# The last down-projection unit and the final norm, computed in two token halves

## The chip, the cores and the metric

The kernel runs on one core of a Trainium2 chip. The number that counts is device time in microseconds, as the median of several runs. TensorE is called PE in the rows (PEld is its weight load), VectorE DVE, ScalarE ACT, GpSimd POOL and the queue that issues the DMAs SP. A name that ends in q (PEldq, DVEq) is the sequencer of that engine.

## The reference

A two-layer encoder trunk on 512 tokens of 1024 features. Each layer ends in a gated MLP whose down-projection is added to the residual `x`; after the second layer there is one more RMSNorm, and its result is the output:

```python
def rms_norm(x, g):
    xf = x.astype(jnp.float32)
    y = xf * lax.rsqrt(jnp.mean(xf * xf, axis=-1, keepdims=True) + EPS)
    return (y * g.astype(jnp.float32)).astype(x.dtype)
...
    for l in range(DEPTH):
...
        h = rms_norm(x, norm_ffn_g[l])
        x = x + conv_ffn(h, ffn_w_up[l], ffn_conv_w[l], ffn_conv_b[l], ffn_w_down[l])
    return rms_norm(x, final_norm_g)
```

## The kernel before

**Layout.** Everything is held with features on the 128 partitions and the 512 tokens along the free dimension: `x` is eight tiles of 128x512. Weights come as packs of four 128x128 tiles through four slots. SP loads `w_raw`, ACT rounds it to `w_hi` (line 516), POOL forms the rest `w_lo` (line 405), and a product is made of three TensorE matmuls per tile pair: `w_hi` with the high part of the input, `w_hi` with its low part, `w_lo` with the high part. All of them go through one helper, line 1106. The inputs of the down-projection are `m_hi` and `m_lo`.

**Units.** A dense unit is one 128-feature output tile, summed in the PSUM bank `dense[n % 2]`. The last down-projection of a layer has eight units of ten weight tiles each, so 30 matmuls of 512 columns per unit. When a unit is done, DVE adds the bank to `x` (line 1087) and counts `evac`; ACT then makes `h_hi` (458) and the square of the tile (466) for the coming norm, and DVE makes `h_lo` (733) and adds the square into `ssq` (741). ACT rounds two more packs after each unit, once the slots' old packs have been consumed; `run_done`, which PE counts at the end of each run of weight tiles, tells it so.

**The layer loop.** Every engine walks through a loop over the two layers (`Fori(0, DEPTH)`), written out at PE line 1178, DVE line 765 and ACT line 506, and jumps back once. Right behind PE's jump come the matmuls of the next layer's first group of units. They wait for the banks: the first for the last unit but one, the second (`dense[1]`) for the last unit's addition.

**The tail.** Behind the loop, PE sums the squares over the features with a matrix of ones: one product for `ssq`, which by then holds tiles 0 to 5, and one each for the squares of tiles 6 and 7, in plain float32 (two passes each), into the bank `M[1]`. ACT turns that into the inverse root by a logarithm and an exponential (lines 477 and 480), DVE scales eight tiles (line 1097), and SP stores each tile as it is ready (line 395). The order is what stands in the code; nothing is scheduled by a planner here.

Of the kernel before, what the change touches and what calls it, by code (L numbers as in the profile page):

```python
# [18 lines left out]
DEPTH = 2  # L19
D, S, P = 1024, 512, 128  # L20
KD = D // P
# [10 lines left out]
SLOTS = 4  # L32
# [53 lines left out]
SEGS, UNIT_END, PACK_END, N_SEGS = segments()  # L86
N_PACKS = len(PACK_END)
SEG0 = 5


SCHEDULE = (
# [103 lines left out]
def build(nc, a, out):  # L195
    f32, f32r = mybir.dt.float32, mybir.dt.float32r
    ALU, ACT, AX = mybir.AluOpType, mybir.ActivationFunctionType, mybir.AxisListType
    with ExitStack() as ctx:
# [109 lines left out]
        bias_loaded, setup_done = sem("bias_loaded"), sem("setup_done")  # L308
        y_ready, stored = sem("y_ready"), sem("stored")

        block = ctx.enter_context(nc.Block())

        def bank(b, parts):
# [8 lines left out]
        def _(sp):  # L322
# [25 lines left out]
            for l in range(DEPTH):  # L348
# [47 lines left out]
            sp.wait_ge(stored, 16 * KD)  # L396


        @block.gpsimd
# [45 lines left out]
        def _(act):  # L445
# [60 lines left out]
            with act.Fori(0, DEPTH) as l:  # L506
# [161 lines left out]
                for half, (g0, ng) in enumerate(HALVES):  # L668
# [35 lines left out]

        @block.vector
        def _(dve):
# [55 lines left out]
                    first_sum(o - 2)  # L762
            dve.wait_ge(c_loaded, 16 * N_CONST_LOADS)
            link(V.tensor_copy(ones_r[:, :], ones[:, :]))
            with dve.Fori(0, DEPTH) as l:
                base[0] = l * DVE_LINKS
                links[0] = 3
                for o in (KD - 2, KD - 1):
                    sum_tile(l * 2, o)
# [287 lines left out]
                for half, (g0, ng) in enumerate(HALVES):  # L1057
                    k0 = links[0]
                    e0 = UNIT_END[U_UP[half] - 1]
                    with dve.Fori(0, ng) as i:  # L1060
                        fi = l * FT + g0 + i
                        if half == 0:
                            dve.wait_ge(rstd_ready, l * 2 + 2)
                        dve.wait_ge(run_done, l * N_SEGS + (SEG0 + e0 + 2) + i * 4)
                        V.tensor_tensor(fpad[:, 2:2 + S], dense[0][:, :], rstd[:, :], ALU.mult).then_inc(evac, 1)  # L1065
                        dve.wait_ge(evac, l * N_EV + (U_UP[half] + 1) + i * 2)
                        dve.wait_ge(f_scaled, fi + 1)
                        ins = V.scalar_tensor_tensor(fy, fpad[:, 1:1 + S], par["fconv"][:, bass.ds(fi * 4 + 1, 1)],  # L1068
                                                     fy, ALU.mult, ALU.add)
# [13 lines left out]
                    links[0] = k0 + ng  # L1083
                    for n in range(U_DN[half], U_DN[half] + 8):
                        o = n - U_DN[half]
                        dve.wait_ge(run_done, l * N_SEGS + (SEG0 + UNIT_END[n]))
                        V.tensor_tensor(x[:, o, :], dense[n % 2][:, :], x[:, o, :], ALU.add).then_inc(evac, 1)  # L1087
                        if half == 1 and o:
                            low_tile(l * 2 + 2, o - 1)
                        if half == 1 and 1 < o < KD - 1:  # L1090
                            sum_tile(l * 2 + 2, o - 1)
                with dve.If(l < DEPTH - 1):
                    low_tile(l * 2 + 2, KD - 1)
                assert links[0] == 3 + DVE_LINKS, links
            dve.wait_ge(rstd_ready, 2 * DEPTH + 1)
            for o in range(KD):
                V.scalar_tensor_tensor(yt[:, o, :], x[:, o, :], par["g"][:, 2 * DEPTH * KD + o:2 * DEPTH * KD + o + 1],  # L1097
                                       rstd[:, :], ALU.mult, ALU.mult).then_inc(y_ready, 1)


        @block.tensor
        def _(pe):
# [75 lines left out]
            with pe.Fori(0, DEPTH) as l:  # L1178
# [297 lines left out]
                for half, (g0, ng) in enumerate(HALVES):  # L1476
                    p0 = SEGS[U_UP[half]][0][0]

                    def up(u, i):

                        runs = [(2 * u + s, l * N_PACKS + (p0 + 2 * u + s) + i * 4, 0, 4 * s, 4) for s in range(2)]
                        unit(u, l * N_EV + (U_UP[half] - 2 + u) + i * 2, runs, *h_src,
                             h_tile(l * 2 + 1) if half == 0 and u == 0 else None)

                    def g_tile(k):

                        if k in (0, ng - 1):
                            pe.wait_ge(f_lo, l * FT + (g0 + ng - 1 + (k > 0)))
                    with pe.Fori(0, ng) as i:
                        if half == 0:  # L1490
                            up(0, i)
                            with pe.If(i < 1):
                                norm(l * 2 + 1, "FNORM", l)
                            up(1, i)
                        else:
                            up(0, i)
                            up(1, i)
                    for n in range(U_DN[half], U_DN[half] + 8):
                        dense_unit(n, m_src(0), g_tile if n == U_DN[half] else None)
            take("NORM", 0, DEPTH)  # L1500
            pe.wait_ge(ssq_added, DEPTH * 14 + KD - 3)
            mm(M[1][:, :], ones[:, :], ssq[:, :], True, False)
            for o in (KD - 2, KD - 1):
                pe.wait_ge(sq_ready, DEPTH * 16 + o + 1)
                ins = mm(M[1][:, :], ones[:, :], sq[:, o % 2, :], False, o == KD - 1)
            ins.then_inc(m_ready[1], 1)

# [145 lines left out]
```

## Time and profile before

| | us |
|---|---|
| median of 3 runs | 1279.43 |
| lowest, highest | 1278.46, 1279.56 |
| the profiled execution's own time | 1278.12 |
| its span, first to last instruction | 1276.2 |
| PE busy / DVE / ACT / POOL, share of the span | 99% / 50% / 45% / 46% |

A row of the timeline has the start in us from the span's beginning, the extent in us, the engine, the line, the instruction, output and inputs, and the number of merged instructions. Matmuls are pipelined, and the extent of one (0.39 us at 512 columns) is longer than the distance to the next, so rates are read from starts.

### The profile page before, as it was taken

What the parts mean: (1) busy time and instruction counts of PE and PEld (TensorE: products, weight loads), DVE (VectorE), ACT (ScalarE), POOL (GpSimd) and SP (SyncE); (2) the same over time, 40 slices, a digit from 0 to 9 for tenths busy, and PEclk for the clock granted to TensorE, in tenths of its full rate; (3) what the DMA queues carried; (4) which work ended last, traced back from release to release, by engine and by line L of the source; (5) the groups of instructions that cost most, each with busy time, mean ns of one, the idle gap of its engine ahead of it and who ended that gap; (6) DMA issues with size and microseconds to landing.
All of it is one profiled execution on the core that took longest, in us unless ns stands there. A gap on an engine that the chain in (4) does not pass through costs nothing.

```text
span 1276.2 us, 21086 instructions
## 1 busy us (share of the span) xinstructions
PE 1257.3 (99%) x6066; PEld 1024.9 (80%) x6066; DVE 638.6 (50%) x962; ACT 571.4 (45%) x910; POOL 588.4 (46%) x438
## 2 busy tenths in 40 slices
PE   7999999999999999999999999999999999999996
PEld 5888878888888888888878887788888888888885
DVE  6859774565544013442248697646645430134423
ACT  6442484564443224443345237754643432244433
POOL 4543432536444445554445335425454444455541
PEclk9999999999999999999999999999999999999999
DMA  6353212233333333333323623313233333333333
GB/s 216 104 151 100 75 57 68 85 89 114 93 97 95 98 95 98 95 95 91 101 84 86 171 67 83 83 47 106 84 111 93 96 99 99 91 99 98 93 96 110
DMA packets 77483, 124.89 MB, mean 98 GB/s; under 512 B 7752, under 2 KB 20456, under 8 KB 77416
## 3 DMA queue, kind: packets, MB, share of 16 engines
q1 hardware_dynamic: 77416, 124.03, 33.8%
q8 instruction: 38, 0.62, 0.2%
q14 instruction: 29, 0.24, 0.1%
HBM read 121.45 MB, written 2.55 MB: 97 GB/s over the span
## 4 chain that ended last, share of the span: by engine, by line
issue 38%; PE 38%; POOL 18%; DVE 2%; POOLq 2%; ACT 1%; DMA 1%; SPq 1%; DVEq 0%; ACTq 0%
PE dense L1106 35%; POOL w_lo L405 18%; PE mix L1106 2%; POOLq L404 1%; POOLq L418 1%; DVE arena L784 1%; DMA w_raw<-in_w 1%; DVE arena L1097 0%; DMA x<-in_xT 0%; ACT h_hi L458 0%; SPq L364 0%; ACT w_hi L516 0%; PE mix L1429 0%; ACT arena L492 0%; SPq L379 0%
## 5 line engine op out<-in xcount | busy, mean ns | idle before, releaser
L405 POOL TENSOR_TENSOR w_lo<-w_raw,w_hi 128x512 fp32r<-128x512 f32 x424 | 579.3, 1381 | 652.1 <-ACT w_hi L516 647.5
L1106 PE MATMUL dense<-h_hi,w_hi 128*128 128x512 f32 x992 | 390.9, 394 | 3.2 <-DVE h_lo L733 2.9
L1106 PE MATMUL dense<-h_lo,w_hi 128*128 128x512 f32 x992 | 386.7, 390 | 0.0
L516 ACT ACTIVATE w_hi<-w_raw 128x512 fp32r<-128x512 f32 x422 | 257.3, 626 | 280.4 <-PE dense L1106 262.5
L1106 PE MATMUL dense<-h_hi,w_lo 128*128 128x512 f32 x992 | 269.9, 390 | 0.0
L1106 PEld LDWEIGHTS dense<-h_hi,w_hi 128*128 128x128 f32 x992 | 186.5, 188 | 45.1 <-issue 5.4
L1106 PEld LDWEIGHTS dense<-h_hi,w_lo 128*128 128x128 f32 x992 | 186.3, 188 | 40.6 <-issue 1.7
L1106 PEld LDWEIGHTS dense<-h_lo,w_hi 128*128 128x128 f32 x992 | 186.5, 188 | 39.5 <-issue 1.4
L1106 PE MATMUL dense<-m_hi,w_hi 128*128 128x512 f32 x544 | 212.9, 391 | 0.0
L1106 PE MATMUL dense<-m_lo,w_hi 128*128 128x512 f32 x544 | 211.8, 389 | 0.0
L1106 PE MATMUL dense<-m_hi,w_lo 128*128 128x512 f32 x544 | 147.7, 389 | 0.0
L1106 PEld LDWEIGHTS dense<-m_hi,w_hi 128*128 128x128 f32 x544 | 102.1, 188 | 21.4
L1106 PEld LDWEIGHTS dense<-m_hi,w_lo 128*128 128x128 f32 x544 | 102.1, 188 | 21.3
L1106 PEld LDWEIGHTS dense<-m_lo,w_hi 128*128 128x128 f32 x544 | 102.1, 188 | 20.9
L1087 DVE TENSOR_TENSOR x<-dense,x 128x512 f32<-128x512 f32 x32 | 22.1, 691 | 191.4 <-PE dense L1106 191.4
L1065 DVE TENSOR_TENSOR arena<-dense,rstd 128x512 f32<-128x512 f32 x44 | 30.4, 692 | 86.0 <-PE dense L1106 86.0
L685 ACT ACTIVATE arena<-arena 128x512 f32<-128x512 f32 x44 | 27.8, 632 | 85.9 <-DVE arena L1072 85.9
L1075 DVE TENSOR_TENSOR arena<-dense,rstd 128x512 f32<-128x512 f32 x44 | 30.4, 691 | 71.4 <-PE dense L1106 71.4
L1068 DVE SCALAR_TENSOR_TENSOR arena<-arena,params 128x512 f32<-128x512 f32 x44 | 35.7, 810 | 59.6 <-ACT arena L680 59.6
L825 DVE TENSOR_TENSOR x<-dense,x 128x512 f32<-128x512 f32 x48 | 33.0, 688 | 56.5 <-PE dense L1106 56.3
L458 ACT ACTIVATE h_hi<-x,params 128x512 fp32r<-128x512 f32 x39 | 28.2, 722 | 69.9 <-DVE x L1087 59.6
L1106 PE MATMUL mix<-arena 64*128 64x128 f32 (+4 forms) x696 | 56.3, 297 | 0.0
(203 smaller groups left out, 1188.1 us busy)
## 6 DMA issues: line engine op xcount, KB each, us to landing
w_raw<-in_w SPq DMA_DIRECT2D x428, 256.0 KB, 2.6
arena<-cum_rows SPq DMA_DIRECT2D x8, 512.0 KB, 6.3
x<-in_xT SPq DMA_DIRECT2D x8, 256.0 KB, 5.1
out_y<-arena SPq DMA_DIRECT2D x8, 256.0 KB, 2.2
arena<-exp_rows SPq DMA_DIRECT2D x12, 128.0 KB, 6.3
consts<-in_consts SPq DMA_DIRECT2D x1, 839.0 KB, 7.1
rel_scratch<-arena SPq DMA_DIRECT2D x1, 382.0 KB
bias<-rel_scratch SPq DMA_DIRECT2D x8, 32.0 KB, 2.3
```

Source lines behind the costliest of these rows:

```text
L404: pool.wait_ge(hi_ready, pack + 1)
L405: nc.gpsimd.tensor_tensor(w_lo[:, s, :], w_raw[:, s, :], w_hi[:, s, :].bitcast(f32), ALU.subtract).then_inc(lo_ready, 1)
L418: with pool.Fori(g0, g1) as i:
L458: nc.scalar.activation(h_hi[:, o, :], x[:, o, :], ACT.Copy, scale=gcol(e, o)).then_inc(h_hi_ready, 1)
L516: nc.scalar.activation(w_hi[:, slot, :], w_raw[:, slot, :], ACT.Copy).then_inc(hi_ready, 1)
L685: nc.scalar.activation(fs, fy, ACT.Silu).then_inc(f_silu, 1)
L825: V.tensor_tensor(x[:, o, :], d[:, :], x[:, o, :], ALU.add).then_inc(evac, 1)
L1065: V.tensor_tensor(fpad[:, 2:2 + S], dense[0][:, :], rstd[:, :], ALU.mult).then_inc(evac, 1)
L1068: ins = V.scalar_tensor_tensor(fy, fpad[:, 1:1 + S], par["fconv"][:, bass.ds(fi * 4 + 1, 1)], fy, ALU.mult, ALU.add)
L1075: V.tensor_tensor(fb, dense[1][:, :], rstd[:, :], ALU.mult).then_inc(evac, 1)
L1087: V.tensor_tensor(x[:, o, :], dense[n % 2][:, :], x[:, o, :], ALU.add).then_inc(evac, 1)
L1106: return T.matmul(dst, lhsT, rhs, start=start, stop=stop)
```

## The change

The last unit of each layer's last down-projection (output tile 7) is computed in two token halves of 256 columns: half 0 into `dense[1]`, half 1 into the bank `M[0]`, each with all 30 matmuls. Half 0 has its own counters (`half_done`, `half_evac`, `half_sq`); `run_done` for these weight runs is counted in half 1 alone. DVE adds the halves separately, and ACT squares them separately.

In layer 0 half 1 stands inside the loop, under a condition on the layer. In the last layer it stands behind the loop, and the sum of squares of half 0 is put in its middle. That sum is now one product over `ssq` (tiles 0 to 6) and one over the square of tile 7, of 256 columns each; half 1's sum follows in bank `M[3]`. ACT takes a square root of each half instead of logarithm and exponential, DVE takes its reciprocal, and then scales the eight tiles of that half. Nine stores of half tiles, seven of them two tiles at a time, replace eight. One addition of squares (tile 6) moves from the head of the next layer to the end of the units.

```diff
-            for o in range(KD):
-                sp.wait_ge(y_ready, o + 1)
-                sp.dma_start(out[o], yt[:, o, :]).then_inc(stored, 16)
+            for c in range(2):
+                for o0, o1 in OUT_DMAS[c]:
+                    sp.wait_ge(y_ready, KD * c + o1)
+                    sp.dma_start(out[o0:o1, :, HALF[c]].rearrange("o p s -> p o s"),
+                                 yt[:, o0:o1, HALF[c]]).then_inc(stored, 16)
...
-                act.wait_ge(evac, l * N_EV + (N_UNITS - 1) + 1)
-                square_tile(l * 2 + 2, KD - 1)
+                act.wait_ge(half_evac, l + 1)
+                act.wait_ge(ssq_added, (l * 2 + 2) * 7 + KD - 3)
+                last_square(0, l, half_sq)
                 with act.If(l < DEPTH - 1):
+                    act.wait_ge(evac, l * N_EV + (N_UNITS - 1) + 1)
+                    last_square(1, l, sq_ready)
                     high_tile(l * 2 + 2, KD - 1)
                     hi_to(N_PACKS + SLOTS - 1)
...
-            rms(4, "NORM", DEPTH)
+            nc.scalar.preload_act_table(ACT.Sqrt)
+            act.wait_ge(m_ready[1], ready("NORM", 0, DEPTH))
+            last_root(0, 1)
+            act.wait_ge(evac, (DEPTH - 1) * N_EV + (N_UNITS - 1) + 1)
+            last_square(1, DEPTH - 1, sq_ready)
+            act.wait_ge(m_ready[3], DEPTH * BANK_TOTAL[3] + 1)
+            last_root(1, 3)
...
+            def inverse(c):
+
+                dve.wait_ge(root_ready, c + 1)
+                V.reciprocal(rstd[:, HALF[c]], rstd[:, HALF[c]]).then_inc(inverse_ready, 1)
+                dve.wait_ge(inverse_ready, c + 1)
...
+            inverse(0)
+            for o in range(2):
+                scaled(o, 0)
+            last_evac(DEPTH - 1)
+            for o in range(2, KD):
+                scaled(o, 0)
+            inverse(1)
             for o in range(KD):
-                V.scalar_tensor_tensor(yt[:, o, :], x[:, o, :], ...
+                scaled(o, 1)
...
+                pe.wait_ge(evac, l * N_EV + N_UNITS - 2)
+                last_half(0, l)
+                pe.wait_ge(m_free[0], (l + 1) * BANK_TOTAL[0] + 1)
+                with pe.If(l < DEPTH - 1):
+                    last_half(1, l)
...
+            last_half(1, DEPTH - 1, first_half_sum)
```

PE, the end of the layer loop (`REGISTER_ALU` and `COMPARE_AND_BRANCH` are the jump back) and what follows, before:

```order
L1106 MATMUL dense1<-m_hi,w_lo 128x512 [waits w_lo_ready]
L1106 MATMUL dense1<-m_hi,w_lo 128x512 x3
L1178 REGISTER_ALU
L1178 COMPARE_AND_BRANCH
L1106 MATMUL mix1<-ssq,consts 128x512 [waits ssq_added,mix1_free]
L1106 MATMUL mix1<-sq,consts 128x512 [waits sq_ready] x2
```

and the same place now (`mix0` is half 1's bank, `mix1` and `mix3` take the sums of squares; the first four rows are the end of half 1 in layer 0):

```order
L1163 MATMUL mix0<-m_hi,w_lo 128x256 x4
L1584 UNCONDITIONAL_BRANCH
L1235 REGISTER_ALU
L1235 COMPARE_AND_BRANCH
...
L1163 MATMUL mix1<-ssq,consts 128x256 [waits ssq_added,mix1_free]
L1163 MATMUL mix1<-sq,consts 128x256 [waits half_squared]
...
L1163 MATMUL mix3<-ssq,consts 128x256 [waits mix3_free]
L1163 MATMUL mix3<-sq,consts 128x256 [waits sq_ready]
```

The matmuls queued in front of the jump are of 256 columns where they were of 512, and the sums of squares stand in and behind half 1.

DVE behind its loop, before:

```order
L765 REGISTER_ALU
L765 COMPARE_AND_BRANCH
L1097 SCALAR_TENSOR_TENSOR arena<-x,params,rstd 128x512 [waits rstd_ready]
L1097 SCALAR_TENSOR_TENSOR arena<-x,params,rstd 128x512 x7
L198 UNCONDITIONAL_BRANCH
```

and now:

```order
L1138 RECIPROCAL rstd<-rstd 128x256 [waits root_ready]
L1143 SCALAR_TENSOR_TENSOR arena<-x,params,rstd 128x256 [waits inverse_ready]
L1143 SCALAR_TENSOR_TENSOR arena<-x,params,rstd 128x256
L1127 TENSOR_TENSOR x<-mix0,x 128x256 [waits run_done]
L1143 SCALAR_TENSOR_TENSOR arena<-x,params,rstd 128x256 x6
L1138 RECIPROCAL rstd<-rstd 128x256 [waits root_ready]
L1143 SCALAR_TENSOR_TENSOR arena<-x,params,rstd 128x256 [waits inverse_ready]
L1143 SCALAR_TENSOR_TENSOR arena<-x,params,rstd 128x256 x7
```

Two reciprocals and half 1's addition have moved in among the scalings, which are sixteen of 256 columns instead of eight of 512.

## Rows read from the trace of the kernel before

**Rows 1.** Page, part 4: the chain that ended last, by engine and line.

```profile
issue 38%; PE 38%; POOL 18%; DVE 2%; POOLq 2%; ACT 1%; DMA 1%; SPq 1%; DVEq 0%; ACTq 0%
```

**Rows 2.** The chain in order of time, from the last units: start, us, what.

```profile
1199.93 62.81 PE dense L1106 x277
...
1262.76 0.70 DVE x L1087
...
1263.57 0.06 ACT sq L466
...
1264.21 1.28 ACT L477
...
1268.17 0.75 DVE arena L1097
```

**Rows 3.** Timeline of PE where layer 0 ends and layer 1 begins.

```profile
634.78 1.07 PE L1106 MATMUL dense<-m_hi,w_lo 128*128 128x512 f32 x4
635.82 0.49 PE L1106 MATMUL dense<-h_hi,w_hi 128*128 128x512 f32 x1
...
636.63 0.50 PE L1106 MATMUL dense<-h_hi,w_hi 128*128 128x512 f32 x1
```

**Rows 4.** PE's sequencer at its layer loop (line 1178): ns min/median/max, first and last start.

```profile
L1178 PEldq COMPARE_BRANCH  x2: 78/1838/3598, 631.7 to 1258.6; - x2
```

**Rows 5.** The same of a short jump, in the loop over the MLP's tiles (line 1492).

```profile
L1492 PEldq COMPARE_BRANCH  x24: 84/208/337, 280.3 to 1024.6; - x24
```

**Rows 6.** DVE's sequencer at its layer loop (line 765).

```profile
L765 DVEq FUSED_REGOPS  x2: 74/74/74, 19.7 to 641.1; - x2
...
L765 DVEq COMPARE_BRANCH  x2: 50/56/62, 638.2 to 1263.2; - x2
```

**Rows 7.** DMA queues from 632.5 to 634.5 us: packets, MB, share.

```profile
q8 instruction: 1, 0.02, 2.9%
```

**Rows 8.** Timeline of PE, matmuls of 128 columns, float32 (one pass each).

```profile
203.14 0.94 PE L1106 MATMUL mix<-arena 128*128 128x128 f32 x7
```

**Rows 9.** Timeline of PE, float32 passes of 512 columns in the tail.

```profile
1262.56 1.02 PE L1106 MATMUL mix<-ssq,consts 128*128 128x512 f32 x2
```

**Rows 10.** Timeline of DVE in the last units and the tail.

```profile
1255.95 0.69 DVE L1087 TENSOR_TENSOR x<-dense,x 128x512 f32<-128x512 f32 x1 [4.85 <-PE dense L1106]
...
1262.76 0.69 DVE L1087 TENSOR_TENSOR x<-dense,x 128x512 f32<-128x512 f32 x1 [4.86 <-PE dense L1106]
...
1268.17 5.39 DVE L1097 SCALAR_TENSOR_TENSOR arena<-x,params,rstd 128x512 f32<-128x512 f32 x8 [4.06 <-ACT rstd L480]
```

**Rows 11.** Groups of DVE by form: xcount, busy us, mean ns, idle before.

```profile
L972 DVE RECIPROCAL den<-den 128x8 f32<-128x8 f32 x8 | 1.6, 203 | 0.3
L861 DVE RECIPROCAL dt_w<-dt_w 128x32 f32<-128x32 f32 x2 | 0.7, 354 | 0.1
L862 DVE TENSOR_TENSOR dt_w<-dt_w,dt_e 128x32 f32<-128x32 f32 x2 | 0.4, 192 | 0.1
L1018 DVE TENSOR_TENSOR arena<-mix,consts 128x256 f32<-128x256 f32 x16 | 6.0, 418 | 0.4 <-PE mix L1106 0.4
L997 DVE SCALAR_TENSOR_TENSOR ssq<-mix,rstdc,consts 128x256 f32<-128x256 f32 x4 | 1.9, 475 | 0.0
```

**Rows 12.** Timeline of ACT in the last unit and the tail.

```profile
1257.94 1.14 ACT L516 ACTIVATE w_hi<-w_raw 128x512 fp32r<-128x512 f32 x2
1263.57 0.63 ACT L466 ACTIVATE sq<-x 128x512 f32<-128x512 f32 x1 [4.49 <-DVE x L1087]
1264.21 1.28 ACT L477 ACT_TABLE_LOAD   x1
1265.51 0.69 ACT L477 ACTIVATE rstd<-mix,params 128x512 f32<-128x512 f32 x1
1266.21 1.28 ACT L480 ACT_TABLE_LOAD   x1
1267.51 0.63 ACT L480 ACTIVATE rstd<-rstd 128x512 f32<-128x512 f32 x1
```

**Rows 13.** The stores, line, engine, KB each, median us from issue to landing.

```profile
out_y<-arena SPq DMA_DIRECT2D x8, 256.0 KB, 2.2
bias<-rel_scratch SPq DMA_DIRECT2D x8, 32.0 KB, 2.3
```

**Rows 14.** Stretches of the tail: us, busy of PE, PEld, DVE, ACT, POOL, then PEclk.

```profile
1266.50:1268.50 2.00, 0.00 (x0) 0.00 (x0) 0.33 (x1) 1.62 (x2) 0.00 (x0) 1.00 0.00 0
...
1270.50:1272.50 2.00, 0.00 (x0) 0.00 (x0) 2.00 (x4) 0.00 (x0) 0.00 (x0) 0.50 1.03 381
```

More of the change, by code:

```diff
@@ L88 @@
 SEG0 = 5
+HALF = (slice(0, S // 2), slice(S // 2, S))
+OUT_DMAS = ((0, 2), (2, 4), (4, 6), (6, 8)), ((0, 2), (2, 4), (4, 6), (6, 7), (7, 8))
 SCHEDULE = (
@@ L309, in build @@
         y_ready, stored = sem("y_ready"), sem("stored")
+        half_done, half_evac, half_sq = sem("half_done"), sem("half_evacuated"), sem("half_squared")
+        root_ready, inverse_ready = sem("root_ready"), sem("inverse_ready")
         block = ctx.enter_context(nc.Block())
@@ L695, in _, with last_square @@
                             norm_tile(l * 2 + 2, n - U_DN[1], l * N_EV + n + 1)
-                act.wait_ge(evac, l * N_EV + (N_UNITS - 1) + 1)
-                square_tile(l * 2 + 2, KD - 1)
+                def last_square(c, layer, done):
+                    nc.scalar.activation(sq[:, 1, HALF[c]], x[:, KD - 1, HALF[c]], ACT.Square).then_inc(done, 1)
+                act.wait_ge(half_evac, l + 1)
+                act.wait_ge(ssq_added, (l * 2 + 2) * 7 + KD - 3)
+                last_square(0, l, half_sq)
                 with act.If(l < DEPTH - 1):
+                    act.wait_ge(evac, l * N_EV + (N_UNITS - 1) + 1)
+                    last_square(1, l, sq_ready)
                     high_tile(l * 2 + 2, KD - 1)
@@ L701, in _, with last_root @@
                 assert links[0] == ACT_LINKS, links
-            rms(4, "NORM", DEPTH)
+            def last_root(c, b):
+                nc.scalar.activation(rstd[:, HALF[c]], M[b][:, HALF[c]], ACT.Sqrt, scale=1.0 / D,
+                                     bias=par["eps"][:, 0:1]).then_inc(root_ready, 1)
+            nc.scalar.preload_act_table(ACT.Sqrt)
[5 more added lines that the diff above has]
+            last_root(1, 3)
         @block.vector
@@ L767, in _ @@
                 links[0] = 3
-                for o in (KD - 2, KD - 1):
-                    sum_tile(l * 2, o)
+                sum_tile(l * 2, KD - 1)
                 def lo_from(dst, src, hi, done):
@@ L1085, in _ @@
                         o = n - U_DN[half]
+                        if half == 1 and o == KD - 1:
+                            low_tile(l * 2 + 2, o - 1)
+                            sum_tile(l * 2 + 2, o - 1)
+                            dve.wait_ge(half_done, l + 1)
+                            V.tensor_tensor(x[:, o, HALF[0]], dense[n % 2][:, HALF[0]], x[:, o, HALF[0]],
+                                            ALU.add).then_inc(half_evac, 1)
+                            continue
                         dve.wait_ge(run_done, l * N_SEGS + (SEG0 + UNIT_END[n]))
@@ L1498, in _ @@
                     for n in range(U_DN[half], U_DN[half] + 8):
[L1499 to L1506, printed above, removed]
+                        if n < N_UNITS - 1:
+                            dense_unit(n, m_src(0), g_tile if n == U_DN[half] else None)
@@ new lines, in last_half @@
+                def last_half(c, layer, between=None):
+                    d = (dense[1], M[0])[c][:, HALF[c]]
+                    for i, (p, t0, k0, m) in enumerate(SEGS[N_UNITS - 1]):
+                        if c == 0:
+                            pe.wait_ge(hi_ready, layer * N_PACKS + p + 1)
+                        for j in range(m):
+                            w = w_hi[:, p % SLOTS, P * (t0 + j):P * (t0 + j) + P]
+                            mm(d, w, m_hi[:, k0 + j, HALF[c]], k0 + j == 0, False)
+                            mm(d, w, m_lo[:, k0 + j, HALF[c]], False, False)
+                        if c == 0:
+                            pe.wait_ge(lo_ready, layer * N_PACKS + p + 1 + SLOTS)
+                        if i == 1 and between is not None:
+                            between()
+                        for j in range(m):
+                            ins = mm(d, w_lo[:, p % SLOTS, P * (t0 + j):P * (t0 + j) + P],
+                                     m_hi[:, k0 + j, HALF[c]], False, k0 + j == HALVES[1][1] - 1)
+                        if c == 1:
+                            ins.then_inc(run_done, 1)
+                    if c == 0:
+                        ins.then_inc(half_done, 1)
@@ new lines, in _, with first_half_sum @@
+                pe.wait_ge(evac, l * N_EV + N_UNITS - 2)
[3 more added lines that the diff above has]
+                    last_half(1, l)
+            def first_half_sum():
+                take("NORM", 0, DEPTH)
+                pe.wait_ge(ssq_added, DEPTH * 14 + KD - 2)
+                mm(M[1][:, HALF[0]], ones[:, :], ssq[:, HALF[0]], True, False)
+                pe.wait_ge(half_sq, DEPTH)
+                mm(M[1][:, HALF[0]], ones[:, :], sq[:, 1, HALF[0]], False, True).then_inc(m_ready[1], 1)
@@ L1510 @@
+            last_half(1, DEPTH - 1, first_half_sum)
+            pe.wait_ge(m_free[3], DEPTH * BANK_TOTAL[3] + 1)
+            mm(M[3][:, HALF[1]], ones[:, :], ssq[:, HALF[1]], True, False)
+            pe.wait_ge(sq_ready, DEPTH * 16 + KD)
+            mm(M[3][:, HALF[1]], ones[:, :], sq[:, 1, HALF[1]], False, True).then_inc(m_ready[3], 1)
 CONSTS = {"ident": P, "ones": P, "sel": 8, "causal": P, "cos": 64 * NB, "sin": 64 * NB,
```

15 lines of the change are left out of this document (11 added, 4 removed).

## The prediction

> **What bounds the kernel now.** Read the chain by engine first [rows 1], then in order of time [rows 2]. Until 1262.7 us nearly all of it is TensorE at work ("issue" stands for the steps between its instructions, and POOL has long shares but no wait of TensorE behind it). What TensorE gains or loses inside the units therefore goes into the time one for one. The end is a different stage: from 1262.76 to 1276.2, 13.4 us, one engine after another works alone: DVE's addition, ACT's square, the last sums, a table load, the logarithm, a second load, the exponential, then 5.4 us of scalings and a store. So the change has two prices, one at each layer's end on TensorE, one in the tail.
>
> **Matmuls of 256 columns.** A unit is 30 matmuls, and the additions behind two units start 6.81 us apart [rows 10]: 0.227 us each at 512 columns, which is 13 ns over 512 columns at 2.4 GHz (0.213). No row shows this kind at 256 columns. From below, matmuls of 128 columns in float32 (two column times each, so as long a stream as 256 columns here), each with its own load of 128 weight columns, start (0.94 − 0.27)/6 = 0.11 us apart [rows 8], so a weight load hides behind a stream of this length. From above, the width may not matter at all: 0.227. A float32 pass of 512 columns takes (1.02 − 0.59)/1 = 0.43 [rows 9], and at 256 columns 0.214, which is nearly the same bound. I take 0.12, half the stream plus the 13 ns, because the weight load was the only reason against it and the nearest row has it hidden. Sixty matmuls then take 7.2 us where thirty took 6.8: **+0.4** per layer.
>
> **The end of layer 0.** This is the term that the diff doesn't show. TensorE's jump back to the loop's head took 3598 ns, from 631.7 on [rows 4], while short jumps take 208 ns [rows 5]. It cost almost nothing, because the sequencer was ahead: matmuls queued before it ran until 635.69 (the last group starts at 634.78, and its fourth at 635.46) [rows 3], that is 4.0 us or 17.6 matmuls. The first matmul of layer 1 starts at 635.82, 4.1 us after the jump began, so 0.13 us were lost, and another 0.36 at 636.63, where `dense[1]` had to be emptied.
>
> Does the jump take this long whatever stands in the queue? DVE's jump at its loop's end starts at 638.2 and its next sequencer step at 641.1, 2.9 us later, with a single instruction still running there [rows 6], and during TensorE's jump one packet of 0.02 MB went through the instruction queue [rows 7]. Both say that the jump waits for code, not for its own queue. The cover is a number of matmuls, and those are now of 256 columns: 17.6 × 0.12 = 2.1 us. TensorE then stands still for 4.1 − 2.1 = 2.0 us; the 0.36 for `dense[1]` goes, since the half's addition ends within 0.8 us of the run. Net 2.0 − 0.49 = **+1.5**. The Trainium skill ("Runtime: NRT & Kernel Launch", Instruction fetch mechanics) has the rule that speaks against this change: a taken branch whose target is outside the two-page window waits for a DMA fetch of the target page. By that rule the stall is as above; without it the branch would go with the queue. The trace agrees with the rule by its 3598 ns.
>
> The condition before half 1 is a short jump (0.2 us) behind a full queue: nothing. ACT's second of the two roundings after the last unit (its slot is freed in half 1 now) comes 3 us later, at about the time its square starts; POOL and SP follow later by as much, with packs that TensorE needs only some 5 us into layer 1. Nothing. The addition of squares moved out of the next layer's head stands in DVE's idle time: nothing. Neither does 2 us without matmuls lower the clock: in the tail it is 1.00 still at 1266.5 to 1268.5, after TensorE's end at 1265.4, and 0.50 only from 1270.5 [rows 14].
>
> **The tail**, on the clock of the trace before. The last unit starts at 1255.75, and half 0 ends 3.6 us later, at 1259.35. Its addition starts 0.2 after that and takes 0.42 [rows 11]. But ACT's queue holds the rounding that waits for the first run of half 1 (1260.3), 0.52 until the next can start [rows 12], then the square of 256 columns, 0.63 − 0.21 = 0.42, to 1261.2. One table load, 1.28, to 1262.5, and the root, 0.69 − 0.21 = 0.48, to 1263.0. The sums of half 0 inside half 1 are ready at 1262.1 and hide behind the table load.
>
> From 1263.0 on DVE is never free, so its queue sets the end:
> - a **reciprocal** of 256 columns: 203 ns at 8 columns and 354 at 32 [rows 11] give 6.3 ns a column and 0.15 fixed, 1.76 us. An ordinary operation of 32 columns takes 192, so this is no ordinary operation. From below 0.42, the price of one of 256 columns; from above 354/32 × 256 = 2.83. I take the line through the two rows. Plus 0.16 for the wait on its result.
> - two scalings, an addition, six scalings. Scalings of 512 columns start (5.39 − 0.75)/7 = 0.663 apart [rows 10]; 256 columns less is 0.27 less (0.745 against 0.475 [rows 11]), 0.395. The addition 0.34. Sum 3.5, to 1268.5.
> - half 1's root must be there: addition to 1266.2, square 0.42, two float32 passes with their latency 0.8, root 0.48: 1267.9, 0.6 us in time.
> - the second reciprocal with its wait, 1.92, seven scalings and the whole of the eighth, 3.25: 1273.7.
>
> Before, scaling ended at 1268.17 + 5.39 = 1273.56. So **+0.1**: what one table load, the half-width sums and the early start give (5.1 us earlier at DVE) goes into 3.8 us for two reciprocals, 0.34 for the addition, and the fixed part of sixteen instructions, 16 × 0.395 against 8 × 0.663, 1.0. The store behind it takes 2.2 at 256 KB and 2.3 at 32 KB [rows 13], so 128 KB gain nothing.
>
> On the reciprocal the rows have only 8 and 32 columns. The Trainium skill ("VectorE: DVE Perf Modes", the list of physical resources) says that it is an iterative divide with a repeat count of 8; as an estimate from that page, 8 cycles at 0.96 GHz are 8.3 ns a column, and the sum would be 1.0 us higher. The rows show 6.3 and not 8.3.
>
> **Sum.** 0.4 + 1.5 + 0.1 = +2.0 us, 0.16%. The profiled execution has 1278.12 (its span 1276.2 and 1.9 around it), the median is 1279.43; nothing around the span changes, so the two should move alike: about 1280.1 and **1281.4**.
>
> **Rivals.**
> - *The reciprocal is ordinary* (0.42). DVE's queue is 2.6 us shorter, half 1's root arrives at 1266.6 and still in time: 1281.4 − 2.6 = 1278.8. Against it: 354 ns where others take 192.
> - *The jump shrinks with its queue*, since 3598 ns is close to 16 matmuls of 0.227. Then only 0.13 is lost at the boundary, 1.9 less: 1279.5. Against it: DVE's 2.9 us without a queue.
> - *The reciprocal is dearer*, up to 2.83: 2.1 more, 1283.5. By the skill's repeat count it would be 1282.5.
> - *The width doesn't matter to TensorE* (0.214 to 0.227). This ends clearly slower: layer 0 takes 6.0 more (the jump is covered again, −0.15), and in the last layer half 1's run ends at 1269.5 instead of 1263.8, its addition holds up DVE's queue, and the end comes 3.9 later: +9.8, 1289.2. It decides from where 60 matmuls run past 1265.8, at 0.15 each.
> - *The halves don't overlap as written*, because half 0's square or sum is late and TensorE waits in the middle of half 1. The square is ready at 1261.2 and TensorE reaches that product at 1261.5, so 0.3 us are spare; a miss of half a microsecond is hidden by DVE's queue.
>
> **How the numbers follow.** The forecast, with its small terms, 0.62, between 1280.4 and 1282.6; ordinary reciprocal 0.08; shrinking jump 0.08; dearer reciprocal 0.08; width without effect 0.09; other mishaps, both gains together among them, 0.05. The range 1278.7 to 1283.5 takes in all but the wide matmuls and the mishaps, some 0.86. About 0.2% is what a measurement can tell from no change: 1276.9 to 1282.0. Faster needs two rivals of gain at once, or a term I don't see: 0.06. Slower: wide matmuls, the dear reciprocal, and the upper fifth of the forecast, 0.30. Same 0.64.
>
> **What would show it.** In the profile after: matmuls of 256 columns 0.12 apart; the long jump on PE's sequencer still some 3.6 us, and TensorE idle about 2.0 us behind half 1 of layer 0 with "issue" as its releaser; layer 1 later by 1.9; `RECIPROCAL` at about 1.76 us; DVE without a gap from the first reciprocal on; the clock at 1.00 across the boundary. A reciprocal under 1.2 us, an idle time under 1 us at the boundary, or an idle DVE in the tail would each make a step of this wrong.

## The result, and the profile after

Median 1281.3 us (1280.0 to 1283.1 over 18 runs) against 1278.49 us (1278.1 to 1279.6, 18 runs): ratio 1.0021, 95% interval 1.0015 to 1.0027. The kernel after is 2.8 us slower. The profiled execution of after took 1281.98 us (span 1280.2), that of before 1278.12 (1276.2): 3.9 more, and 4.0 in the spans. Three executions in experiments 1 and 2 (1404.56, 4809.79 and 1408.69 us) were in a slow state and are left out of every median and comparison.

Where these 4.0 us stand is read at one point: the start of the last unit of the last layer. Timeline of PE, first before and then after, at this point (start us, us, what):

```profile
1255.75 0.39 PE L1106 MATMUL dense<-m_hi,w_hi 128*128 128x512 f32 x1
```

```profile
1259.96 0.28 PE L1163 MATMUL dense<-m_hi,w_hi 128*128 128x256 f32 x1
1260.08 0.28 PE L1163 MATMUL dense<-m_lo,w_hi 128*128 128x256 f32 x1
```

So 4.2 us are lost ahead of this unit, and the tail gives 0.2 back. The matmuls of 256 columns start 0.12 us apart.

All but 0.2 of the 4.2 us is lost where layer 0 ends. The last unit of layer 0 starts only 0.16 us later than before (timelines of PE, before and after):

```profile
628.89 0.39 PE L1106 MATMUL dense<-m_hi,w_hi 128*128 128x512 f32 x1
```

```profile
629.05 0.28 PE L1163 MATMUL dense<-m_hi,w_hi 128*128 128x256 f32 x1
```

PE's sequencer at its layer loop (the row that answers to [rows 4]), then the timeline of PE (that of [rows 3]):

```profile
L1235 PEldq COMPARE_BRANCH  x2: 76/2098/4121, 634.2 to 1261.9; - x2
```

```profile
635.76 0.64 PE L1163 MATMUL mix<-m_hi,w_lo 128*128 128x256 f32 x4
638.81 0.79 PE L1163 MATMUL dense<-h_hi,w_hi 128*128 128x512 f32 x1 [2.41 <-DVE h_lo L758]
639.40 0.63 PE L1163 MATMUL dense<-h_lo,w_hi 128*128 128x512 f32 x1
639.83 0.63 PE L1163 MATMUL dense<-h_hi,w_hi 128*128 128x512 f32 x1
...
643.26 0.39 PE L1163 MATMUL dense<-h_hi,w_hi 128*128 128x512 f32 x1
```

Two things are to be seen. First the gap: the fourth matmul of the last group starts at 635.76 + 3 × 0.12 = 636.1, the next one at 638.81, where before the distance was 0.36 [rows 3]. PE's weight loads name the sequencer itself as what they waited for (list of waits from 630 to 645 us: us in total, times, longest):

```profile
PEld dense L1163 <- issue: 2.6, 1, 2.6
```

(The row puts 2.41 down to DVE's `h_lo`, whose last tile is written from 638.06 to 638.81, so it ends just as the matmul starts. That is no proof of a wait: in the first experiment below the same matmul, with the same waits, starts at 636.30, 2.6 us before that tile is written.) Second, behind the gap matmuls of 512 columns start 0.43 us apart instead of 0.227, and the rows say why. Stretches of the same place, PE alone: us, busy, PEclk, DMA share, GB/s:

```profile
636.00:637.00 1.00, 0.40 (x4) 1.00 0.29 47
637.00:638.00 1.00, 0.00 (x0) 1.00 0.61 215
638.00:639.00 1.00, 0.19 (x1) 0.92 0.02 8
639.00:640.00 1.00, 1.00 (x3) 0.50 0.13 33
...
642.00:643.00 1.00, 1.00 (x5) 0.87 0.38 102
```

From 638.9 to 642.3 the granted clock is 0.50, that is 1.2 GHz instead of 2.4. In these 3.4 us TensorE did the work of about 1.7; by the starts, the twelve matmuls from 638.81 to 643.26 took 4.45 us where the same ones take 2.85 in experiment 2 at a clock of 1.00. In the profile of before there is no such stretch at this place. So the 4.2 us are 0.2 (ahead of the unit) + 0.4 (narrower matmuls) + 2.1 (idle 2.6 where before 0.13 and 0.36 were lost) + 1.6 (the clock).

The tail, timeline of DVE after (answers to [rows 10]):

```profile
1263.76 0.42 DVE L1115 TENSOR_TENSOR x<-dense,x 128x256 f32<-128x256 f32 x1 [0.38 <-PE dense L1163]
1267.23 1.75 DVE L1138 RECIPROCAL rstd<-rstd 128x256 f32<-128x256 f32 x1 [3.05 <-ACT rstd L718]
1269.02 0.88 DVE L1143 SCALAR_TENSOR_TENSOR arena<-x,params,rstd 128x256 f32<-128x256 f32 x2
1269.82 0.42 DVE L1127 TENSOR_TENSOR x<-mix,x 128x256 f32<-128x256 f32 x1
1270.15 2.46 DVE L1143 SCALAR_TENSOR_TENSOR arena<-x,params,rstd 128x256 f32<-128x256 f32 x6
1272.52 1.75 DVE L1138 RECIPROCAL rstd<-rstd 128x256 f32<-128x256 f32 x1
1274.31 3.26 DVE L1143 SCALAR_TENSOR_TENSOR arena<-x,params,rstd 128x256 f32<-128x256 f32 x8
```

From 1267.23 on no row has an idle time in front: DVE's queue sets the end. Scaling ends 1277.57 − 1259.96 = 17.61 us after the unit's start; before it was 1273.56 − 1255.75 = 17.81.

### The profile page after: what moved, and what is told of

Same layout as the page of the kernel before. It is cut to its first block, busy times and chain, and to the rows that moved or that the text cites. A ratio compares the mean times of both kernels' runs of the same rounds, so it can differ in the third digit from the quotient of the medians.

```text
span 1280.2 us, 21226 instructions
## 1 busy us (share of the span) xinstructions
PE 1258.8 (98%) x6128; PEld 1029.9 (80%) x6128; DVE 642.6 (50%) x975; ACT 569.9 (45%) x911; POOL 587.9 (46%) x438
## 4 chain that ended last, share of the span: by engine, by line
issue 38%; PE 37%; POOL 18%; DVE 2%; POOLq 2%; ACT 1%; DMA 1%; SPq 1%; DVEq 0%; ACTq 0%
PE dense L1163 35%; POOL w_lo L411 18%; PE mix L1163 2%; POOLq L410 1%; DMA w_raw<-in_w 1%; POOLq L424 1%; DVE arena L809 1%; DVE arena L1143 0%; DMA x<-in_xT 0%; ACT h_hi L464 0%; DVE rstd L1138 0%; ACT w_hi L522 0%; SPq L368 0%; PE mix L1486 0%; ACT arena L498 0%
## 5 line engine op out<-in xcount | busy, mean ns | idle before, releaser
L1163 PE MATMUL dense<-m_hi,w_hi 128*128 128x512 f32 (+1 forms) x544 | 210.2, 387 | 0.0
L1163 PE MATMUL dense<-m_lo,w_hi 128*128 128x512 f32 (+1 forms) x544 | 209.1, 385 | 0.0
L1163 PE MATMUL dense<-m_hi,w_lo 128*128 128x512 f32 (+1 forms) x544 | 145.6, 385 | 0.0
```

The costliest lines, as they stand in the source:

```text
L1163: return T.matmul(dst, lhsT, rhs, start=start, stop=stop)
```

## Experiments

Theory A: everything lost stands at the layer boundary, because PE's long jump is no longer covered by matmuls in the queue, and the clock falls because of the standstill. The rivals are B, the narrow matmuls themselves lower the clock; C, the loss has another place or cause; and, for the tail, that another chain than DVE's queue sets the end. Times are medians; each stands beside runs of the kernel before on the same chip.

**1. No jump.** TensorE's loop over the layers is written out; everything else is the kernel after.

```diff
-            with pe.Fori(0, DEPTH) as l:
+            for l in range(DEPTH):
...
-                with pe.If(l < DEPTH - 1):
+                if l < DEPTH - 1:
```

> The kernel after, with TensorE's two layers written out one behind the other instead of a loop, so that its queue has no long jump at the layer boundary; every matmul, wait and bank is as in the kernel after. Theory A (the time went to the jump, and the fall of the clock follows from the stall): the idle 2.6 us at the boundary go to under 0.3, the matmuls behind it run 0.227 apart from the start (granted clock 1.00 throughout), and the time is 1281.3 - 2.6 less 0 to 1.7 = 1277.0 to 1278.7, at or below the kernel before. Rival B (the 48 narrow matmuls lower the clock, whatever stands behind them): the idle goes, but the clock still falls to half for some 3.4 us, 1278.7 and a spread of 3 us over the runs. Rival C (the time is lost elsewhere, in the rounding or the squares behind the halves): the first matmul of the second layer waits for a rounded tile instead, and the time stays at 1281.

Measured: 1277.78 us against 1278.45 before, ratio 0.9994 (0.9984 to 1.0003). Timeline of PE at the boundary:

```profile
635.82 0.64 PE L1163 MATMUL mix<-m_hi,w_lo 128*128 128x256 f32 x4
636.30 0.40 PE L1163 MATMUL dense<-h_hi,w_hi 128*128 128x512 f32 x1
...
636.98 0.50 PE L1163 MATMUL dense<-h_hi,w_hi 128*128 128x512 f32 x1
```

The first matmul of layer 1 follows 0.12 us behind the last of layer 0, so nothing that it needs was late; only the third starts 0.2 us later than it could. The clock is 1.00 across the boundary, behind the same 60 narrow matmuls (the expectation's 48 is a slip). Theory A holds; C doesn't, nor does B as long as TensorE doesn't stand still. Against the kernel after this is 3.5 us, more than the price of the jump alone (2.6), as it must be if the clock goes too. That the jump waits for code is not measured directly, but one row fits: from 634.2 to 638.3 us the instruction queue q8 moved one packet of 0.02 MB in the profile of after, and none in this one.

**2. Halves in layer 0 alone.** The tail is that of the kernel before. The edit brings in `last_half` with PE's condition and DVE's and ACT's parts for layer 0, and keeps the whole unit behind the loop:

```diff
+                with pe.If(l < DEPTH - 1):
+                    pe.wait_ge(evac, l * N_EV + N_UNITS - 2)
+                    last_half(0, l)
+                    pe.wait_ge(m_free[0], (l + 1) * BANK_TOTAL[0] + 1)
+                    last_half(1, l)
+            l = DEPTH - 1
+            runs = [(p % SLOTS, l * N_PACKS + p, t0, k0, m) for p, t0, k0, m in SEGS[N_UNITS - 1]]
+            unit(1, l * N_EV + N_UNITS - 3, runs, *m_src(0))
```

> The kernel before, with the last down-projection unit of the first layer alone in two token halves and two banks; final norm, scalings and stores are those of the kernel before, with the last unit in one piece. Theory A: everything that makes the kernel after slower is here: 0.4 us of narrower matmuls, 2.1 to 2.5 us of idle time behind the long jump instead of 0.13 and a wait of 0.36 that goes, and 0 to 1.7 us from a lowered clock; 1278.5 + 2.0 to 4.1 = 1280.5 to 1282.6. Rival C (the tail gives what was lost): 1278.5 to 1279.0.

Measured: 1282.16 us, ratio 1.0027 (1.0017 to 1.0036): the whole loss is here, 3.7 us where the whole change costs 2.8, a difference within the intervals. The timeline of PE, and the jump's row:

```profile
637.10 0.64 PE L1125 MATMUL mix<-m_hi,w_lo 128*128 128x256 f32 x4
639.82 0.49 PE L1125 MATMUL dense<-h_hi,w_hi 128*128 128x512 f32 x1 [2.08 <-ACT w_hi L518]
```

```profile
L1197 PEldq COMPARE_BRANCH  x2: 76/1934/3791, 635.5 to 1257.3; - x2
```

In this profile the jump took 3.79 us and left 2.1 to 2.3 us idle, and the clock stayed at 1.00. It took 1281.65, but 1.2 us of that had been lost in the first 50 us of the program already (PE was busy for 42.24 of them, against 43.42 in the profile of after). Such a difference at the start is part of every single time here.

**3. Halves in the last layer alone.**

```diff
-                pe.wait_ge(evac, l * N_EV + N_UNITS - 2)
-                last_half(0, l)
-                pe.wait_ge(m_free[0], (l + 1) * BANK_TOTAL[0] + 1)
                 with pe.If(l < DEPTH - 1):
-                    last_half(1, l)
+                    dense_unit(N_UNITS - 1, m_src(0))
...
+            pe.wait_ge(evac, (DEPTH - 1) * N_EV + N_UNITS - 2)
+            last_half(0, DEPTH - 1)
+            pe.wait_ge(m_free[0], DEPTH * BANK_TOTAL[0] + 1)
             last_half(1, DEPTH - 1, first_half_sum)
```

> The kernel after, with the last unit of the first layer in one piece and one bank as in the kernel before; the last layer's unit, the final norm, the scalings and the stores are by halves, as in the kernel after. Theory A: the tail alone is worth what the profile after shows from the last unit's start to the end, 20.24 us instead of 20.45: 1278.5 - 0.2 = 1278.3, with the boundary as in the kernel before (idle 0.13 us, clock at 1.00). By the prediction's own sum of the tail it is 1278.6. Rival C (the tail loses time, or the loss at the boundary has another cause than the narrow matmuls ahead of the jump): over 1279.5.

Measured: 1278.06 us, 0.4 below before, ratio 0.9996 (0.9987 to 1.0004): the expected gain is not told from none. With experiment 2 the change is split into its two parts, +3.7 and −0.4; their sum, 3.3, is 0.5 above the measured 2.8.

**4. The jump covered by other matmuls.**

```diff
                 with pe.If(l < DEPTH - 1):
                     last_half(1, l)
+                    pe.wait_ge(m_free[5], (l + 1) * BANK_TOTAL[5] + 1)
+                    for _ in range(9):
+                        mm(M[5][:, :], ones_r[:, :], m_hi[:, 0, :])
```

> The kernel after, with nine matmuls of 512 columns more at the end of the first layer, between the second half of the last unit and the jump; they write a free bank that nobody reads. They take 9 x 0.227 = 2.0 us and cover the jump: the last 17.6 matmuls ahead of it then last 9 x 0.227 + 8.6 x 0.12 = 3.1 us instead of 2.1. Theory A (the clock falls since TensorE stands still too long): the idle time falls from 2.6 to 1.6 us, the matmuls behind it keep 0.227 us and the clock 1.00; 2.0 - 1.0 = 1.0 us more work on the path, less 0 to 1.7 for the clock: 1280.6 to 1282.3, with less spread between runs than the kernel after. Rival B (the narrow matmuls lower the clock): the clock falls as in the kernel after, behind or in the nine matmuls, and the time is 1282.3 or more, with the same spread.

Measured: 1281.02 us, ratio 1.002 (1.0012 to 1.0029), ten of eleven runs within 1.2 us. Timeline of PE, and the jump's row:

```profile
635.74 0.64 PE L1163 MATMUL mix<-m_hi,w_lo 128*128 128x256 f32 x4
636.22 2.25 PE L1163 MATMUL mix<-m_hi,ones_r 128*128 128x512 f32 x9
639.12 0.50 PE L1163 MATMUL dense<-h_hi,w_hi 128*128 128x512 f32 x1 [0.64 <-ACT w_hi L522]
```

```profile
L1235 PEldq COMPARE_BRANCH  x2: 76/1726/3376, 635.3 to 1260.6; - x2
```

Two microseconds of work that nobody needs cost nothing against the median of the kernel after, in part because the clock doesn't fall: against the nine fastest of its eighteen runs (median 1280.33) they cost 0.7. The gap shrinks from 2.4 to 0.64 and the clock stays at 1.00. The jump was issued with 3.0 us of matmuls queued (635.3 to 638.3), close to the 3.1 reckoned from 17.6 matmuls, but it was shorter than expected, 3.38 instead of 4.1. The releaser in the row is again not what counts: the first matmul starts 0.44 us behind the jump's end here, 0.49 in the profile of after and 0.53 in experiment 2, while the row names `w_hi` or `h_lo`.

**5. Shorter reciprocals.** Experiment 3 with 32 columns of each half inverted instead of 256. The kernel leaves out the inverse of the other 448 columns, so it only serves to read a time.

```diff
-                V.reciprocal(rstd[:, HALF[c]], rstd[:, HALF[c]]).then_inc(inverse_ready, 1)
+                few = slice(256 * c, 256 * c + 32)
+                V.reciprocal(rstd[:, few], rstd[:, few]).then_inc(inverse_ready, 1)
```

> The run in which only the last layer's unit is in halves, with both reciprocals over 32 of their 256 columns; the other 448 columns of the scalings are then multiplied by the root and not by its inverse, so this part of the computation is left out. In that run a reciprocal of 256 columns took 1.75 us, and one of 32 columns takes 0.35 by the rows of before. Theory D (DVE's queue sets the end from the first root on): both differences go into the time, 2 x 1.40 = 2.8 us: 1278.06 - 2.8 = 1275.3. Rival E (another chain, the unit's end and half 1's root, is close behind, and takes over): the first reciprocal's gain is swallowed while DVE waits for half 1's root, and only 1.4 us are gained: 1276.7. Rival F (the store or the end of the program sets the time): 1278.

Measured: 1275.15 us against 1278.31 before, ratio 0.9976 (0.9967 to 0.9985). That is 3.2 below before; experiment 3 was 0.4 below, so 2.8 us less, the whole difference of both reciprocals. The timeline of DVE shows it filled again from the first reciprocal to the end:

```profile
1263.22 0.35 DVE L1138 RECIPROCAL rstd<-rstd 128x32 f32<-128x32 f32 x1 [3.05 <-ACT rstd L716]
1263.61 0.88 DVE L1143 SCALAR_TENSOR_TENSOR arena<-x,params,rstd 128x256 f32<-128x256 f32 x2
...
1264.75 2.45 DVE L1143 SCALAR_TENSOR_TENSOR arena<-x,params,rstd 128x256 f32<-128x256 f32 x6
1267.12 0.34 DVE L1138 RECIPROCAL rstd<-rstd 128x32 f32<-128x32 f32 x1
1267.49 3.26 DVE L1143 SCALAR_TENSOR_TENSOR arena<-x,params,rstd 128x256 f32<-128x256 f32 x8
```

**6 and 7. Logarithm and exponential by halves, and the same without the jump.** If DVE's reciprocals are what eats the gain of the halves, the inverse root should stay on ACT, for all its table loads. Layer 0 is that of experiment 3. Two things change in the tail at once: where the inverse root is made, and half 1's addition, which moves ahead of the first scaling.

```diff
-                nc.scalar.activation(rstd[:, HALF[c]], M[b][:, HALF[c]], ACT.Sqrt, scale=1.0 / D,
+                nc.scalar.activation(rstd[:, HALF[c]], M[b][:, HALF[c]], ACT.Ln, scale=1.0 / D,
                                      bias=par["eps"][:, 0:1]).then_inc(root_ready, 1)
+                nc.scalar.preload_act_table(ACT.Exp)
+                act.wait_ge(root_ready, c + 1)
+                nc.scalar.activation(rstd[:, HALF[c]], rstd[:, HALF[c]], ACT.Exp,
+                                     scale=-0.5).then_inc(inverse_ready, 1)
...
-                V.reciprocal(rstd[:, HALF[c]], rstd[:, HALF[c]]).then_inc(inverse_ready, 1)
...
+            last_evac(DEPTH - 1)
             inverse(0)
-            for o in range(2):
+            for o in range(KD):
                 scaled(o, 0)
-            last_evac(DEPTH - 1)
```

> The run in which only the last layer's unit is in halves, with the logarithm and the exponential of the kernel before for each half, on ACT, in place of root and reciprocal: ACT has four table loads of 1.28 us instead of one, DVE has no reciprocal, and half 1's addition stands ahead of the first scaling. From the rows of the other run: half 0's sum at 1262.5, logarithm 0.5, load 1.28, exponential 0.5, scaling from 1264.9 on (1265.1 with the reciprocal); eight scalings of half 0 to 1268.1; half 1's square at 1265.3, load, logarithm, load, exponential to 1268.7; eight scalings, 3.25, to 1272.0 instead of 1273.6. Theory D (the reciprocals stand in the queue that sets the end, the loads do not): 1278.06 - 1.6 = 1276.4. Rival G (four loads on ACT are the longer chain): half 1's exponential comes after 1270.3, and the time is 1278.1 or more.

> The same as the run with logarithm and exponential by halves in the last layer, with TensorE's two layers written out one behind the other. The jump is gone and with it the 0.13 us that it cost before; DVE's addition for the last unit is still waited for. Theory A: 0.1 to 0.4 us less than that run, about 1276.2, with the granted clock at 1.00 across the boundary. Rival H (straight code is fetched as slowly as a jump's target, somewhere else): as that run or later, with idle time of TensorE by "issue" at other places.

Measured: 1276.54 us, ratio 0.9986 (0.9977 to 0.9995), and 1276.12 us, ratio 0.9984 (0.9975 to 0.9993). Both are faster than the kernel before, by 1.8 and 2.2 us, and than the kernel after by about 5, most of which is the undone halves of layer 0. Against experiment 3, each beside its own runs of before, the new tail is worth 1.4; the addition's own 0.34 us in DVE's queue is part of that, and no run separates the two. Timeline of DVE, and of ACT for half 1, in the first of the two:

```profile
1264.26 0.42 DVE L1130 TENSOR_TENSOR x<-mix,x 128x256 f32<-128x256 f32 x1 [4.02 <-PE mix L1166]
1265.03 3.25 DVE L1145 SCALAR_TENSOR_TENSOR arena<-x,params,rstd 128x256 f32<-128x256 f32 x8 [0.34 <-ACT rstd L720]
1268.85 3.26 DVE L1145 SCALAR_TENSOR_TENSOR arena<-x,params,rstd 128x256 f32<-128x256 f32 x8 [0.57 <-ACT rstd L720]
```

```profile
1265.32 1.28 ACT L731 ACT_TABLE_LOAD   x1
1266.61 0.47 ACT L716 ACTIVATE rstd<-mix,params 128x256 f32<-128x256 f32 x1
1267.11 1.28 ACT L718 ACT_TABLE_LOAD   x1
1268.40 0.42 ACT L720 ACTIVATE rstd<-rstd 128x256 f32<-128x256 f32 x1
```

DVE now waits 0.57 us for half 1's exponential, so ACT's chain has just become the bound, and the two are nearly even. The second kernel's 0.4 us less agree with the expected 0.1 to 0.4, but their intervals overlap.

**8. A standstill behind wide matmuls.** Experiment 3 without the jump, and with a wait in its place:

```diff
+                if l:
+                    pe.wait_ge(h_lo_ready, l * 16 + 8)
```

> The run in which only the last layer's unit is in halves, with TensorE's layers written out (no jump) and one wait more: before its first matmul of the second layer TensorE waits until DVE has written the low part of the last tile. By the rows of that run TensorE's last matmul ahead of it ends at 636.2 and the low part at 639.1: 2.9 us of standing still, behind matmuls of 512 columns, none of 256. Without a change of the clock the price is 2.9 - 0.3 = 2.6 us on 1278.06 - 0.2, that is 1280.4. Theory A (a stall of this length lowers the clock, whatever the matmuls ahead): the granted clock falls to 0.50 for some 3.4 us, matmuls 0.43 us apart, 1.7 us more, in some runs or in all: 1280.4 to 1282.1, a spread of 1 us or more. Rival B (the narrow matmuls are needed for the fall): 1.00 throughout, 1280.4, with a spread under 0.5 us.

Measured: 1281.98 us (1280.48 to 1282.21, 7 runs), ratio 1.0029 (1.0018 to 1.004). The profiled execution is the one of 1280.48, with the clock at 1.00 behind a standstill of 2.94 us (timeline of PE, then a stretch: us, busy, PEclk, DMA share, GB/s):

```profile
638.99 0.50 PE L1165 MATMUL dense<-h_hi,w_hi 128*128 128x512 f32 x1 [2.94 <-DVE h_lo L759]
```

```profile
639.00:640.00 1.00, 1.00 (x4) 1.00 0.05 16
```

The other six are 1.3 to 1.7 above it. What they had the times alone don't tell, so one more profile of it was taken, and one more of the kernel after.

**9 and 10. After, and the standstill, once more.**

> The kernel after once more, for one more profile of the boundary. Its times spread from 1280.0 to 1283.1 where those of the kernel before keep within 1.5 us. Theory A: the idle time behind the jump is there in every run, 2 to 2.6 us, and the clock falls behind it in some only: with granted clock 1.00 from 639 to 643 the time is 1280.0 to 1280.7, with 0.50 it is 1281.5 to 1283. Rival I (the spread comes from the start of the program, whose first 100 us hold the waits for weights): the clock is as in the first profile, and the difference stands in the first 100 us.

> The kernel with the stall of 2.9 us behind matmuls of 512 columns once more. Its profiled execution had the clock at 1.00 behind the stall and took 1280.5, its six other runs 1281.7 to 1282.2. Theory A: those six had the fallen clock, so a profile that shows 1281.7 or more has 0.50 in its rows for some 3.4 us and matmuls 0.43 apart, and one with 1.00 has 1280.5. Rival B (512-column matmuls ahead of the stall keep the clock up): 1.00 in this profile too, whatever the time.

Measured: 1282.71 and 1283.60 us. Stretches of the kernel after (the first two rows) and of the standstill (its timeline of PE, then stretches):

```profile
640.00:641.00 1.00, 1.00 (x5) 0.59 0.03 8
...
642.00:643.00 1.00, 1.00 (x4) 0.50 0.67 217
```

```profile
635.10 1.07 PE L1165 MATMUL dense<-m_hi,w_lo 128*128 128x512 f32 x4
639.12 0.79 PE L1165 MATMUL dense<-h_hi,w_hi 128*128 128x512 f32 x1 [2.94 <-DVE h_lo L759]
```

```profile
638.00:639.00 1.00, 0.00 (x0) 0.73 0.03 8
639.00:640.00 1.00, 0.89 (x2) 0.50 0.06 16
...
644.00:645.00 1.00, 1.00 (x4) 0.50 0.02 8
645.00:646.00 1.00, 1.00 (x6) 0.86 0.00 0
```

In the standstill's profile the clock is at 0.50 from 638.5 to 645.3, behind nothing but matmuls of 512 columns: rival B falls. Of this stretch 6.2 us are work, at half speed, so about 3.1 us are lost, and 1280.48 + 3.1 = 1283.6 is what was measured. The two profiles of one kernel also show that at this length of standstill the fall comes in some executions only: the same 2.94 us, once without it and once with it. What decides between them, no run shows. The expected length of the lowered stretch was 3.4 us; it was twice that.

Rival I is right in part: the kernel after took 0.7 us more than in its first profile with the same gap (2.41) and the same 3.4 us at 0.50; its jump was issued at 634.9 instead of 634.2, and the same DVE row (L809) starts at 44.69 instead of 44.01, so those 0.7 us were lost in the first 45 us. The fall itself came later here, at 640.2, when TensorE had been at work again for 0.7 us.

**11. A standstill of 6 us.** Experiment 8 with a later signal to wait for; the diff is against experiment 8.

```diff
-                    pe.wait_ge(h_lo_ready, l * 16 + 8)
+                    pe.wait_ge(ssq_added, l * 14 + 7)
```

> As the stall of 2.9 us, but TensorE waits for DVE's last sum of squares ahead of the second layer, which ended at 642.3 in the run with only the last layer in halves: a stall of 6.1 us, 3.2 more. Theory A (standing still lowers the clock, the surer the longer): 0.50 in every execution, in rows behind the stall or already in it; time 1280.5 + 3.2 = 1283.7, and 0 to 1.7 more, as much of the lowered stretch as falls on work. Rival B (the narrow matmuls are needed): 1283.7 with 1.00 in all rows behind the stall.

Measured: 1285.58 us (1285.06 to 1286.4, 4 runs), ratio 1.0059 (1.0042 to 1.0076). In the profile TensorE stands still for 6.08 us, until 641.78; the clock falls in this time and is low when work begins:

```profile
638.00:639.00 1.00, 0.00 (x0) 0.81 0.02 8
639.00:640.00 1.00, 0.00 (x0) 0.50 0.07 16
...
642.00:643.00 1.00, 1.00 (x3) 0.50 0.82 170
645.00:646.00 1.00, 1.00 (x5) 0.78 0.00 0
```

The time is 1283.7 and 1.9 more, 0.2 above the upper end of theory A; none of the four runs is as low as 1283.7. That a longer standstill makes the fall surer fits, but one profile doesn't prove it.

## Why the prediction was right, and where not

The forecast was 1281.4 us and the measured time is 1281.3. The agreement is closer than the reasoning was. The forecast added 2.0 us to a median of 1279.43 from three runs; eighteen runs give 1278.49, and the difference measured is 2.8. The start was 0.9 too high and the sum 0.8 too low, and the two cancel by luck. There is luck in the median too. Of the eighteen runs of after, nine lie between 1280.0 and 1281.04 (median 1280.33) and nine between 1281.55 and 1283.1 (median 1282.02); the median of all, 1281.3, lies in the gap between the groups, where no run was. The ratio of 1.0021 stands on the bound of 0.2% that the prediction drew between same and slower.

- **Matmuls of 256 columns**, 0.12 us apart, +0.4: measured 0.12. The nearest row (matmuls of 128 columns in float32 with their own weight loads) was the right one. *The width doesn't matter* is refuted.
- **The jump is not covered any more.** The mechanism is shown by experiments 1, 2 and 4; its place, the end of layer 0, was named. By rule and row: the Trainium skill ("Runtime: NRT & Kernel Launch", Instruction fetch mechanics) has a taken branch to a target outside the current window wait for the fetch of the target page. The rows agree so far as the jump did not shrink with its queue: 4.1 us with 2.0 us of matmuls queued, 3.4 with 3.0, 3.6 with 4.0. The size was off: 4.1 us instead of 3.6, so the idle time was 2.6 instead of 2.0, and the net loss 2.1 instead of 1.5. The mis-sized term was "the long jump on PE's sequencer still some 3.6 us", one row of one execution. The rival *the jump shrinks with its queue* is refuted.
- **The clock** was the step that failed: "Neither does 2 us without matmuls lower the clock". It was argued from the tail, where 0.50 came only some 5 us behind TensorE's end [rows 14]. That row shows where the clock fell in one place of one execution; it is no bound for another standstill. Experiments 8 and 10 show 2.9 us of standstill with the fall and without it, and experiment 2 2.1 us without it. In the profile of after it costs 1.6 us, where the forecast put nothing, on a sum of 2.0. That the upper nine runs are those with the fall is suggested by experiments 8 to 10, since both profiles of after, 1281.98 and 1282.71, have it; by the distance of the groups' medians, 1.7 us; and by the mean granted clock listed with each execution, which is 0.995 in seven of the upper nine and 0.996 in two, but 0.996 to 0.998 in the lower nine (means 0.9952 and 0.9967; 3.4 us at half clock in 1280 are 0.0013, and the tail's low stretch counts in all of them). No profile of the lower group was taken, so it isn't shown directly.
- **ACT, POOL, SP and the moved sum**, no cost: right. Experiment 1 keeps all of them, and its first matmul of layer 1 has no wait; the third has one of 0.2 us, on DVE's addition of half 1, which in the kernel after is hidden behind the jump, as forecast.
- **Half 0's root**: DVE's first reciprocal was to start 1263.0 − 1255.75 = 7.25 us behind the unit's start. Measured 1267.23 − 1259.96 = 7.27. The rival *the halves don't overlap* is refuted.
- **The reciprocal**, 1.76 us by the line through 8 and 32 columns: measured 1.75. Both rivals on its price are refuted. The estimate from the Trainium skill's repeat count ("VectorE: DVE Perf Modes", the list of physical resources) was 8.3 ns a column; from 32 to 256 columns the rows have 6.2, and the measurement decides.
- **DVE's queue sets the end**: shown by experiment 5, whose 2.8 us came through in full. In size the tail was 0.3 too dear (+0.1 forecast, −0.2 measured), nearly all of it the wait for the reciprocal's own result, 1.79 together instead of 1.92, twice.

## What to carry to other kernels

A long backward jump of TensorE costs nothing only as long as the matmuls queued ahead of it last longer than the jump takes (3.4 to 4.1 us here); whoever shortens the matmuls in front of it, by splitting them or making them narrower, pays for the jump, so count the cover in microseconds and not in instructions, or write the loop out. A standstill of 2.4 us or more can cost more than itself, since the clock may fall and stay low behind it. When a serial tail is split in two so that its halves overlap, look at the engine that both halves queue on: a reciprocal that ran beside nothing before is added to that queue twice, and here the slower looking pair of functions on the idle engine was the better one.

## What the runs showed of the hardware that was not expected

- The granted clock of TensorE fell from 2.4 to 1.2 GHz (1.00 to 0.50) during or up to 0.7 us behind standstills of 2.4 us (both profiles of after), 2.94 us (one of two profiles) and 6.1 us, and did not fall with 0.6 us, 2.1 us and the other 2.94 us. It stayed low for 3.4 us in the two profiles of after, and for 6.8 us in experiments 10 and 11, though TensorE was at work again without a pause.
- The long jump of PE took 3.60 us in the profile of before, 4.12 in both profiles of after, and 3.79, 3.39, 3.38, 3.83 and 3.57 in experiments 2 to 6: its length varies by 0.7 us from kernel to kernel without following the queue (with about 3.9 us queued it was 3.39 to 3.83). The kernel after has the same 4.12 in both its profiles, so it may belong to the program rather than to the execution. What it follows is open.
